# The border into the attention mixer: two chunks on the raw residual, the RMS root in the heads' norms

## Chip, cores and metric

One core of a Trainium2 chip runs the whole program in one launch. The metric is the device time of that core in microseconds; a comparison goes by the median of several runs.

## The reference, cut to what matters

Two blocks run one after the other on a residual x of 512 tokens by 1024 features. The first block ends with a post-norm (a LayerNorm), and the second begins with an RMS norm in front of its attention mixer:

```python
def _layer_norm(x, gain, bias):
    mu = jnp.mean(xf, -1, keepdims=True)
    var = jnp.mean(jnp.square(xf - mu), -1, keepdims=True)
    return (xf - mu) * lax.rsqrt(var + LN_EPS) * gain + bias
...
x = _post_norm(x, y, g3, FFN_RES, ln_gain[l, 2], ln_bias[l, 2])   # l = 1: end of the first block
...
def rmsnorm(x, g):
    return xf * lax.rsqrt(jnp.mean(xf * xf, axis=-1, keepdims=True) + EPS) * g
...
h = rmsnorm(x, g_mix[0])                                          # start of the second block
qa, ka, va, qb, ckv, qi, ki, wi = _split(h @ w_in, EVEN_SPLITS)
qa = rope(rmsnorm(qa, gq_a)); ka = rope(rmsnorm(ka, gk_a))        # by heads of 64
kb, vb = jnp.split(rmsnorm(ckv, g_kv_b) @ w_kv_up_b, 2, axis=-1)
qb = rope(rmsnorm(qb, gq_b)); kb = rope(rmsnorm(kb, gk_b))
qi = rope(qi); ki = rope(rmsnorm(ki, g_kidx)); wi = wi * (IDX_HEADS ** -0.5 * IDX_DIM ** -0.5)
```

The index scores relu(qi ki) weighted by wi choose, for every token, which keys the second half of the heads sees (the k_sel highest). A positive factor common to all scores of a token doesn't alter that choice. A head's norm removes a common factor of its input, but for its eps.

## The kernel before, in words

The residual stands transposed: XR holds 8 tiles of 128 features by 512 tokens. A chunk is 256 output columns of a weight matrix (1024 KB). SyncE loads it into one of three stage buffers, ScalarE rounds it to the high part WH (`split`), VectorE forms the low part WL (`low`), and each product is three matmuls (high x high, high x low, low x high; `mul3`) of 128 rows by 512 columns, for eight steps of k. The input of the projections is kept as a high and a low part too: HH and HL, or for the hidden layer AH and AL.

A planner (class Plan, from line 80 on) writes one list of steps; every engine then runs its own part of each step in the order of that list. `feat` and `mm2` emit a chunk's matmuls, and after every few of them `tick` (L613) lets each active generator add its next step, so that attention units, rotations and top-k rounds are spread between matmuls. `until` (L626) ticks without adding matmuls of weights until a condition holds. Temporary buffers, PSUM banks and small buffers are rings; a buffer taken again carries the event that must be over first.

Five borders of the first block use `late` (L325). While the last down projection writes the residual, `raw` (xg) scales each tile by gain times modulation into AH[1] and AL[1]. Two chunks then multiply this unnormalised residual, with a column sum of the stage's weights against two coefficient columns (`weight_sums`, L1449) after each step of k. Between these matmuls run the mean (`ln_mean`), its subtraction and the squares (`ln_sub`), the variance (`ln_var`), the root by three Newton steps (`ln_root`, twelve short VectorE instructions in `rsqrt`, L2036) and its spread over a bank (`ln_spread`). `ln_h` scales the residual and makes HH and HL, and `late_copy`, `uv_out` and `late` correct the two chunks' outputs by mean and root. `scaled` later brings XR to its final value, one tile per tick (`ln_x`).

The border into the attention mixer has no such overlap. `last_norm` (L453) computes mean, subtraction, squares, variance, root and the final residual with a second set of squares (steps ln_a and ln_last; `keep` puts nine matmuls without use into TensorE's waits). `rms_norm` (L491) then makes the mixer's root (rms_a) and h (rms_b). After it `even_mixer` (L857) projects the chunk w_kiwi (128 columns of ki twice, 4 of wi), then w_in_e 7 (qi). The squares of ki are summed (e_stat) and group(0), the norm and rotation of ki, is started behind the first half of qi: a root (g_rs), its transposes (g_turn), the scaling (g_scale) and the rotation (e_rope). `until` waits for ki; then index() (scores and top-k) and the projections of qa, ka, va follow.

## Time and profile before

| | us |
|---|---|
| median of 3 runs | 3678.25 (3675.61 to 3683.49) |
| the profiled execution | 3687.77 |
| its span, first to last instruction | 3686.4 |
| mean granted clock of TensorE | 0.974 |
| busy in the span: PE, PEld, DVE, ACT, POOL | 3572.3, 2904.3, 1882.5, 1219.3, 492.4 |

In the profile PE is TensorE's matmuls, PEld its weight loads (beside the matmuls), DVE is VectorE, ACT ScalarE, POOL GpSimd. A granted clock of 1.00 is 2.4 GHz and of 0.50 is 1.2 GHz. The end of a matmul is modelled, so the start-to-start distance of neighbours tells more than their duration.

### The profile page before, as it was taken

What the parts mean: (1) busy time and instruction counts of PE and PEld (TensorE: products, weight loads), DVE (VectorE), ACT (ScalarE), POOL (GpSimd) and SP (SyncE); (2) the same over time, 40 slices, a digit from 0 to 9 for tenths busy, and PEclk for the clock granted to TensorE, in tenths of its full rate; (3) what the DMA queues carried; (4) which work ended last, traced back from release to release, by engine and by line L of the source; (5) the groups of instructions that cost most, each with busy time, mean ns of one, the idle gap of its engine ahead of it and who ended that gap; (6) DMA issues with size and microseconds to landing.
All of it is one profiled execution on the core that took longest, in us unless ns stands there. A gap on an engine that the chain in (4) does not pass through costs nothing.

```text
span 3686.4 us, 41474 instructions
## 1 busy us (share of the span) xinstructions
PE 3572.3 (97%) x16954; PEld 2904.3 (79%) x16954; DVE 1882.5 (51%) x3255; ACT 1219.3 (33%) x1638; POOL 492.4 (13%) x432
## 2 busy tenths in 40 slices
PE   8999989999999999999999998987999999999999
PEld 7888866787888888867788886755888888888887
DVE  4545743664456454644653335686553434664333
ACT  2222461351224222552342223234442223343221
POOL 1010220110002000221110011100211111201111
PEclk9999999899999999999999998987999999999999
DMA  6444222133442444211132221100312222222221
GB/s 251 160 160 154 98 72 89 46 114 125 160 149 98 154 160 140 101 69 69 46 113 101 94 86 49 66 23 3 116 56 102 92 103 95 103 80 92 92 103 69
DMA packets 52608, 373.44 MB, mean 101 GB/s; under 512 B 5826, under 2 KB 5954, under 8 KB 9539
## 3 DMA queue, kind: packets, MB, share of 16 engines
q1 hardware_dynamic: 52418, 370.79, 28.0%
q8 instruction: 134, 2.20, 0.2%
q14 instruction: 56, 0.45, 0.0%
HBM read 368.67 MB, written 2.10 MB: 101 GB/s over the span
## 4 chain that ended last, share of the span: by engine, by line
PE 44%; DVE 4%; ACT 1%; issue 1%; POOL 0%; DVEq 0%; ACTq 0%; POOLq 0%
PE ps L1384 43%; PE ps L1409 0%; ACT s_tmp L1905 0%; DVE s_tmp L2346 0%; DVE s_tmp L2473 0%; DVE s_sm L2453 0%; DVE s_tmp L2336 0%; DVE s_sm L2344 0%; DVE s_bm L2455 0%; DVE s_tmp L2490 0%; DVE s_sm L2324 0%; DVE s_hl L2058 0%; ACT s_wh L1743 0%; DVE s_xx L2346 0%; DVE s_tmp L2486 0%
## 5 line engine op out<-in xcount | busy, mean ns | idle before, releaser
L1384 PE MATMUL ps<-s_hh,s_wh 128*128 128x512 f32 (+1 forms) x2584 | 1028.1, 398 | 16.7 <-POOL s_hl L2610 9.5
L1384 PE MATMUL ps<-s_hl,s_wh 128*128 128x512 f32 (+1 forms) x2584 | 1012.7, 392 | 0.0
L1384 PE MATMUL ps<-s_hh,s_wl 128*128 128x512 f32 (+1 forms) x2584 | 1012.5, 392 | 0.0
L2065 DVE TENSOR_TENSOR s_wl<-s_stage,s_wh 128x2048 fp32r<-128x2048 f32 (+2 forms) x278 | 625.4, 2250 | 625.8 <-ACT s_wh L1743 625.6
L1743 ACT ACTIVATE s_wh<-s_stage 128x2048 fp32r<-128x2048 f32 (+1 forms) x276 | 518.9, 1880 | 622.3 <-PE ps L1384 502.0
L1384 PEld LDWEIGHTS ps<-s_hh,s_wh 128*128 128x128 f32 (+1 forms) x2584 | 488.2, 189 | 141.5 <-issue 39.6
L1384 PEld LDWEIGHTS ps<-s_hh,s_wl 128*128 128x128 f32 (+1 forms) x2584 | 487.8, 189 | 104.8 <-issue 0.2
L1384 PEld LDWEIGHTS ps<-s_hl,s_wh 128*128 128x128 f32 (+1 forms) x2584 | 488.7, 189 | 101.4 <-issue 2.2
L1384 PE MATMUL ps<-s_ah,s_wh 128*128 128x512 f32 x1376 | 547.1, 398 | 0.0
L1384 PE MATMUL ps<-s_ah,s_wl 128*128 128x512 f32 x1376 | 537.4, 391 | 0.0
L1384 PE MATMUL ps<-s_al,s_wh 128*128 128x512 f32 x1376 | 537.0, 390 | 0.0
L2659 POOL TENSOR_TENSOR s_al<-s_tmp,s_ah 128x512 fp32r<-128x512 f32 x152 | 197.6, 1301 | 1691.6 <-ACT s_ah L1743 1691.6
L1384 PEld LDWEIGHTS ps<-s_ah,s_wl 128*128 128x128 f32 x1376 | 258.9, 188 | 54.8
L1384 PEld LDWEIGHTS ps<-s_al,s_wh 128*128 128x128 f32 x1376 | 259.4, 189 | 52.2 <-issue 1.2
L1384 PEld LDWEIGHTS ps<-s_ah,s_wh 128*128 128x128 f32 x1376 | 259.4, 189 | 52.1 <-issue 1.2
L1743 ACT ACTIVATE s_ah<-s_tmp 128x512 fp32r<-128x512 f32 x152 | 96.1, 632 | 587.6 <-DVE s_tmp L2267 328.2
L2118 DVE TENSOR_TENSOR s_xr<-ps,s_xr 128x512 f32<-128x512 f32 x96 | 66.1, 689 | 196.8 <-PE ps L1384 196.7
L2116 DVE SCALAR_TENSOR_TENSOR s_xr<-ps,s_sm,s_xr 128x512 f32<-128x512 f32 x112 | 83.8, 749 | 158.0 <-PE ps L1384 157.4
L2081 DVE SCALAR_TENSOR_TENSOR s_tmp<-s_stage,s_cond,s_tmp 128x256 f32<-128x256 f32 x381 | 156.3, 478 | 0.0
L1767 ACT ACTIVATE s_tmp<-ps 128x512 f32<-128x512 f32 x82 | 48.9, 597 | 267.2 <-PE ps L1384 267.2
L2267 DVE TENSOR_TENSOR s_tmp<-s_tmp,ps 128x512 f32<-128x512 f32 x82 | 56.2, 686 | 155.5 <-PE ps L1384 155.5
L1384 PEld LDWEIGHTS ps<-s_cc,s_tmp 128*128 128x128 f32 x764 | 103.0, 208 | 20.5 <-POOL s_tmp L2650 6.7
(434 smaller groups left out, 3752.4 us busy)
## 6 DMA issues: line engine op xcount, KB each, us to landing
s_stage<-in_w_ada SPq DMA_DIRECT2D x64, 1024.0 KB, 4.8
s_stage<-in_ffn_w_gate SPq DMA_DIRECT2D x44, 1024.0 KB, 4.8
s_stage<-in_ffn_w_up SPq DMA_DIRECT2D x44, 1024.0 KB, 4.8
s_stage<-in_ffn_down SPq DMA_DIRECT2D x32, 1024.0 KB, 4.8
s_stage<-in_w_up SPq DMA_DIRECT2D x32, 1024.0 KB, 4.7
s_stage<-in_down_m SPq DMA_DIRECT2D x32, 1024.0 KB, 4.8
s_stage<-in_w_in SPq DMA_DIRECT2D x24, 1024.0 KB, 4.8
s_stage<-in_ffn_down SPq DMA_DIRECT2D x16, 768.0 KB, 4.3
```

What stands on the lines that cost most here:

```text
L1384: return pe.matmul(out, lhs, rhs, start=start, stop=stop, skip_group_check=True)
L1743: return act.activation(out, src, ACT.Copy)
L1767: act.activation(m.tmp(q), m.bank(b), ACT.Silu).then_inc(*e.up("act_ffn", "act", pid))
L2065: ins = dve.tensor_tensor(m.WL[:, ws, a:z], m.STAGE[:, j % NS, a:z], m.WH[:, ws, a:z].bitcast(F32), ALU.subtract)
L2081: ins = dve.scalar_tensor_tensor(dst, w[:, k, :], cond, dst, ALU.mult, ALU.add)
L2116: ins = dve.scalar_tensor_tensor(x, m.bank(b), m.small(gate[0])[:, n:n + 1], x, ALU.mult, ALU.add)
L2118: ins = dve.tensor_tensor(x, m.bank(b), x, ALU.add)
L2267: dve.tensor_tensor(m.tmp(q), m.tmp(q), m.bank(b), ALU.mult).then_inc(*e.up("dve_ffn", "glu", pid))
L2659: pool.tensor_tensor(m.AL[a][:, k, :], m.tmp(q), m.AH[a][:, k, :].bitcast(F32), ALU.subtract).then_inc(*e.up("pool_a", "a.lo", av, k))
```

## The change

- At the border into the attention mixer `last_norm` and `rms_norm` are replaced: the last down projection prepares the raw residual with gain times g_mix (`ln_coef2`), and `late` does the two chunks w_kiwi (128 and 4 rows, `wide`) and w_in_e 7 on it.
- `late` is given `xq`: after each half of `ln_h`, ScalarE squares the final residual (scale and bias in the instruction) and GpSimd sums the squares (`ln_xq`).
- The mixer's h is only LayerNorm output times g_mix. The RMS root of a token isn't multiplied in. For the heads' norms it goes into their eps: mean of squares plus eps becomes eps of the head times (mean square of x plus eps) (`e_root`, small buffer ew, first four columns). For va it is a scale of the copies (`e_tcopy`, one copy per token tile, two in place of one). For the indexer it is left out, being a common factor.
- ki, wi and qi come out of `e_late`; ki's group waits for ew. The tiles of the mixer change their place in memory, as AH[1] and AL[1] now hold the raw residual while ki, qi and wi are written.

```diff
     def late(self, norm, names, wide=(P, P), xq=False):
...
-        qs = self.to_h()
-        self.add("ln_h", sid, rs, s, self.hfree, self.hv, qs, 0, 4)
-        finish(0, mean, rs)
+        self.add("ln_h", sid, rs, s, self.hfree, self.hv, self.to_h(0, 4), 0, 4)
+        sq = self.squared(sid, s, 0, None) if xq else None
+        finish(one, 0, mean, rs)
         part(1, *two, 4, 8)
-        self.add("ln_h", sid, rs, s, self.hfree, self.hv, qs, 4, NT)
+        self.add("ln_h", sid, rs, s, self.hfree, self.hv, self.to_h(4, NT), 4, NT)
+        sq = self.squared(sid, s, 4, sq[:1]) if xq else None
         self.release(two[0], ("proj", two[1] + 1))
         low = self.ahead()
         copies(two, 1)
...
+    def squared(self, sid, s, n0, acc):
+        qs = [self.tmp.take() for _ in range(1 if not acc else 0)]
+        acc = acc or qs
+        for n in range(n0 + len(qs), n0 + 4):
+            q = self.tmp.take()
+            qs.append(q)
+            self.tmp.free(q, ("ln.xf", sid, n))
+        self.add("ln_xq", sid, s, n0, qs, acc[0])
+        return acc
...
-    def even_mixer(self):
+    def even_mixer(self, norm):
...
+        def root(sq):
+            rid, y, b = self.new(), self.yr.take(), self.held.take()
+            yield
+            self.add("rms_a", rid, sq, b, y)
+            for q, _ in sq:
+                self.tmp.free(q, ("rms.st", rid))
+            self.add("e_root", rid, b, y, ew)
+            self.held.free(b, ("ew",))
+            self.yr.free(y, ("ew",))
+            done["ew"] = True
...
+        self.pipeline()
+        one, two, free, sq = self.late(norm, (("w_kiwi", 0), ("w_in_e", 7)), (P, 4), True)
+        hv, ew = self.hv, self.small.take()
...
         self.add("e_begin")
-        ch = self.take("w_kiwi", 0)
-        b, pid = self.feat(ch, 8, 132, 0, "h", hv)
...
+        for (key, t), (q, pid, su, col) in zip((("ki", 0), ("wi", 0), ("qi", 0), ("qi", 1)), one + two):
+            wi = self.tmp.take() if key == "wi" else None
+            self.add("e_late", key, t, pid, q, su, col, wi)
+            self.tmp.free(q, ("wi.c",) if key == "wi" else ("e.p", key, t))
+            if key == "ki":
+                q = self.tmp.take()
+                self.add("e_sq", key, t, None, q)
+                pend.append((q, key, t, 0))
+            elif key == "wi":
...
+        flush()
+        self.active.append(root(sq))
+        self.bg.append(lambda: "ew" in done)
+        self.bg.append(group(0, 2, [("ki", 0)]))
         self.until(lambda: ("ki", 0) in done)
...
-        total = self.last_norm(1, 2, norm)
         assert not self.fill
         self.pipeline()
...
-                self.rms_norm("g_mix", l, total)
-                self.even_mixer()
+                self.even_mixer(norm)
...
+    def ln_xq(sid, s, n0, qs, acc):
+        AG, AB = m.small(s)[:, 16:24], m.small(s)[:, 24:32]
+        for n in range(n0, n0 + 4):
+            e.wait_ge(("ln.sc", sid, n), qs[n - n0].after)
+            act.activation(m.tmp(qs[n - n0]), m.XR[:, n, :], ACT.Square, bias=AB[:, n:n + 1], scale=AG[:, n:n + 1]).then_inc(
+                *e.up("act_sq", "ln.xq", sid, n))
...
+    def e_tcopy(c, i, pid, b, ew):
+        e.wait_ge(("proj", pid), ("ew",))
+        for a in range(2):
+            ins = act.activation(m.t["va"][:, i + a, 256 * c:256 * c + 256], m.bank(b)[:, 256 * a:256 * a + 256], ACT.Copy,
+                                 scale=m.small(ew)[:, 4 + i + a:5 + i + a])
+        ins.then_inc(*e.up("act_evict", "va", c, i))
...
+    def e_root(rid, b, y, ew):
+        e.wait_ge(ew.after)
+        dve.tensor_scalar(m.small(ew)[:, 0:4], m.bank(b)[:, 0:4], 1e-6, 1e-12, ALU.mult, ALU.add).then_inc(
+            *e.up("dve_e", "ew.a"))
+        e.wait_ge(("rs", rid))
+        dve.tensor_copy(m.small(ew)[:, 4:8], m.y(y)[:, 0:4]).then_inc(*e.up("dve_e", "ew"))
+        e.wait_ge(("ew",))
...
+    def g_rs(gid, n, y, ready, ew):
+        own = 8 if gid == 2 else n
+        v, (src, w) = m.NV[:, 0:4 * n].rearrange("p (a n) -> p a n", a=4), spans((0, own), m.small(ew)[:, 0:4])
+        e.wait_ge(ready, last_rs[0])
+        ins = dve.tensor_tensor(v[:, :, 0:own], src, w, ALU.add)
+        if own < n:
+            ins.then_inc(*e.up("dve_rs", "rs.own", gid))
+            ins = dve.tensor_scalar(v[:, :, own:n], m.t["st"][:, :, own:n], 1e-6, None, ALU.add)
+        ins.then_inc(*e.up("dve_rs", "rs.v", "g%d" % gid))
+        newton("g%d" % gid, 4 * n, y)
...
+    def ln_xq(sid, s, n0, qs, acc):
+        for n in range(max(n0, 1), n0 + 4):
+            e.wait_ge(("ln.xq", sid, n), ("ln.xf", sid, n - 1) if n > 1 else ("ln.xq", sid, 0))
+            pool.tensor_tensor(m.tmp(acc), m.tmp(acc), m.tmp(qs[n - n0]), ALU.add).then_inc(*e.up("pool_sum", "ln.xf", sid, n))
```

## Rows read from the trace of the kernel before

**Rows 1.** The page's part 1, busy time, share of the span and instructions of each engine.

```profile
PE 3572.3 (97%) x16954; PEld 2904.3 (79%) x16954; DVE 1882.5 (51%) x3255; ACT 1219.3 (33%) x1638; POOL 492.4 (13%) x432
```

**Rows 2.** Windows: length, busy us of PE, PEld, DVE, ACT, POOL, clock, DMA share, GB/s.

```profile
2203.05:2237.12 34.07, 21.82 (x97) 18.05 (x96) 22.89 (x52) 18.21 (x27) 6.45 (x6) 0.64 0.08 31
2237.12:2267.40 30.28, 28.66 (x116) 19.65 (x117) 11.87 (x26) 10.26 (x13) 5.01 (x4) 0.89 0.10 35
1502.45:1535.17 32.72, 32.72 (x188) 28.17 (x186) 27.06 (x47) 16.51 (x21) 7.68 (x6) 1.00 0.10 34
```

**Rows 3.** Timeline of PE, border: start us, duration us, instruction, [idle before <-releaser].

```profile
2203.04 1.02 PE L1384 MATMUL ps<-s_tmp,s_cc 128*128 128x512 f32 x2
2225.02 5.28 PE L1384 MATMUL ps<-s_cc,s_tmp 128*128 128x1 f32 x24 [6.42 <-POOL s_tmp L2650]
2237.12 0.77 PE L1384 MATMUL ps<-s_hh,s_wh 128*128 128x512 f32 x1 [2.32 <-DVE s_hl L2058]
2243.37 0.39 PE L1384 MATMUL ps<-s_hh,s_wh 128*128 128x512 f32 x1
```

**Rows 4.** Timeline of PE around the first projection of qa.

```profile
2263.25 0.60 PE L1635 MATMUL ps<-s_cc,s_ny 128*2 128x128 f32 x4
2264.62 1.12 PE L1384 MATMUL ps<-s_rt,s_c 2*128 2x512 f32 x2 [0.77 <-DVE s_rt L2414]
2266.58 1.81 PE L1384 MATMUL ps<-s_ki,s_cc 128*128 128x512 f32 x2 [0.84 <-DVE s_ki L2424]
2267.40 1.42 PE L1384 MATMUL ps<-s_hh,s_wh 128*128 128x512 f32 x1
2268.61 0.63 PE L1384 MATMUL ps<-s_hl,s_wh 128*128 128x512 f32 x1
2270.32 0.40 PE L1384 MATMUL ps<-s_hh,s_wl 128*128 128x512 f32 x1
```

**Rows 5.** Timeline of PE at the border at 1502 us.

```profile
1502.45 0.39 PE L1384 MATMUL ps<-s_ah,s_wh 128*128 128x512 f32 x1
1503.59 0.39 PE L1384 MATMUL ps<-s_ah,s_wl 128*128 128x512 f32 x1
1535.17 0.37 PE L1384 MATMUL ps<-s_wh,s_hh 128*128 128x256 f32 x1
1539.82 0.58 PE L1384 MATMUL ps<-s_wh,s_hh 128*128 128x256 f32 x1 [1.18 <-POOL s_hl L2610]
```

**Rows 6.** Timeline of DVE behind the chunks of that border.

```profile
1540.25 2.29 DVE L2065 TENSOR_TENSOR s_wl<-s_stage,s_wh 128x2048 fp32r<-128x2048 f32 x1 [2.15 <-ACT s_wh L1743]
1545.23 0.88 DVE L2262 TENSOR_SCALAR s_sq<-s_tmp,s_sm 128x512 f32<-128x512 f32 x2
1546.03 0.88 DVE L2262 TENSOR_SCALAR s_sk<-s_tmp,s_sm 128x512 f32<-128x512 f32 x2
```

**Rows 7.** ACT and POOL there by timeline, L1811 by line (min/median/max ns).

```profile
1538.26 1.89 ACT L1743 ACTIVATE s_wh<-s_stage 128x2048 fp32r<-128x2048 f32 x1
...
1538.49 1.27 POOL L2610 TENSOR_TENSOR s_hl<-s_tmp,s_hh 128x512 fp32r<-128x512 f32 x1 [1.08 <-ACT s_hh L1815]
...
L1811 ACT ACTIVATE s_tmp<-s_xr,s_sm x40: 800/814/819, 433.8 to 1865.6; 128x512 f32<-128x512 f32 x40
```

**Rows 8.** By line: GpSimd's sums of squares, ns min/median/max.

```profile
L2640 POOL TENSOR_TENSOR s_tmp<-s_tmp x15: 1282/1290/1302, 417.7 to 1840.1; 128x512 f32<-128x512 f32 x15
```

**Rows 9.** Timeline of DVE: first and last of the 12 steps of a root.

```profile
2230.34 0.16 DVE L2040 TENSOR_SCALAR s_nv<-ps 128x4 f32<-128x4 f32 x1 [4.22 <-PE ps L1384]
2232.51 0.16 DVE L2053 SCALAR_TENSOR_TENSOR s_ny<-s_nu,s_ny 128x4 f32<-128x4 f32 x1
```

**Rows 10.** Timelines of PE and DVE: wi's transposes and their copy.

```profile
2257.34 0.41 PE L1649 MATMUL ps<-s_cc,s_tmp 4*128 4x4 f32 x4
...
2257.79 0.17 DVE L2435 COPY s_wi<-ps 128x16 f32<-128x16 f32 x1 [0.17 <-PE ps L1649]
```

**Rows 11.** Windows: the sum over 2410 to 2570 us.

```profile
sum 160.00, PE 130.42 PEld 81.58 DVE 123.66 ACT 70.53 POOL 15.67; mean PE 32.61 PEld 20.40 DVE 30.91 ACT 17.63 POOL 3.92
```

More of the change, by code:

```diff
@@ L391, in late @@
         copies(two, 1)
-        self.add("uv_out", sid, two[0], 1, uv, su)
         if low:
             self.add("low", *low)
-        finish(1, mean, rs)
+        finish(two, 1, mean, rs)
         self.held.free(uv, ("uv.out", sid, 1))
@@ L525, in ffn @@
                 if first and norm:
-                    one, two, afree[1] = self.late(norm, ((names["gate"], idx), (names["up"], idx)))
+                    one, two, afree[1], _ = self.late(norm, ((names["gate"], idx), (names["up"], idx)))
                     for (q, pid, su, col), (r, pid2, *_) in zip(one, two):
@@ L577, in ffn @@
                 if gi == len(groups) - 1 and mean and not after and not raw:
-                    self.total(mean, *total, done[:-2] if c < 3 else done)
+                    self.total(*total, done[:-2] if c < 3 else done)
                     done = done[-2:] if c < 3 else []
@@ L604, in project_out @@
             if not after and not raw:
-                self.total(mean, *total, done if last else done[:-2])
+                self.total(*total, done if last else done[:-2])
             done = done[-2:]
@@ L759, in dil_units @@
                         yield self.attend("dil", l, 2 * pr + c, i, (i + 1) * P, cell, i == 3 and c == 1)
-        one, two, free = self.late(norm, (("w_in", l * 12 + 9), ("w_in", l * 12 + 10)))
+        one, two, free, _ = self.late(norm, (("w_in", l * 12 + 9), ("w_in", l * 12 + 10)))
         for key, tiles in (("sq", one), ("sk", two)):
@@ L1400, in spread @@
         return ins
-    def keep(b, n):
-        for _ in range(n):
-            mul(b[:, 0:256], m.ident, m.CC[:, 0:256])
     def turn(b, src, n):
```

318 lines of the change are left out of this document (109 added, 209 removed).

## Prediction

> **What bounds the kernel now.** I read the page first: TensorE is busy for 97% of the span and nothing else is above 79% [rows 1]. So only places where TensorE waits, does extra work or runs at its lower clock can move the time, and the change touches one of them, the border from the last feed-forward block to the attention mixer. The table by windows comes next. From the last down projection (2203.05) to the mixer's first projection (2237.12) lie 34.07 us, in which TensorE counts as busy for 21.82 at a granted clock of 0.64; to the first projection of qa (2267.40) it is another 30.28 [rows 2]. The timeline of TensorE says what is in the first stretch: statistics, waits such as the 6.42 us for GpSimd's sum, and no projection [rows 3]. Together that is 64.36 us from 2203.04 to 2267.40, of which the projections of ki, wi and qi need only 96 matmuls at 0.228 = 21.9 (five spacings from 1502.45 to 1503.59 [rows 5]). The border loses about 42 us.
>
> The same trace holds five borders of the other kind, where two chunks multiply the unnormalised residual while the norm is computed. The fourth, at 1502 us, has the same sizes as the new one: 512 columns, eight steps of k, a first and a second chunk with column sums. From its first matmul at 1502.45 to its last column sum TensorE is never idle: 32.72 us, busy 32.72, clock 1.00 [rows 2, 5]. What follows there, a value projection, begins at once at 1535.17. These rows are the yardstick.
>
> **Part by part.** Time is counted from the last down projection, before at 2203.04, in the yardstick at 1502.45.
>
> (a) The whole of last_norm and rms_norm goes, with its nine filler matmuls (keep), and the chunk of ki and wi and the chunk of qi are done as late chunks. The four-row half of the first costs what 128 rows cost, in both kernels, since 512 columns stream through. Cost: 32.72 [rows 2, 5]. The border's upkeep inside it (column sums, mean, variance, spread) is the 10.8 above 21.9. The extra work of the down projection (the scaled residual on ScalarE and VectorE) hid under the yardstick's matmuls, and does so here.
>
> (b) Behind the chunks everything hangs on one chain. even_mixer calls until(ki done) before it emits qa's projection, and until only ticks: it adds no matmul of weights. Before, group 0 (norm and rotation of ki) was started while qi was still multiplying; now ki's group waits for a root of the sum of squares, and that for the late norm. So TensorE has nothing to hide this chain with, and each link counts.
>
> - ScalarE: its split of the next weights started at 1538.26, right after the last copies of the norm [rows 7]. Four squares with scale and bias now stand ahead of it, about 0.81 each like L1811 [rows 7]. Their fourth reuses a buffer that GpSimd frees with its first sum; that sum follows the low part at 1538.49 (1.27) and takes 1.29 [rows 7, 8], so it ends at 1541.1 and the square at about 1541.8. Shift: 3.5.
> - VectorE's low part stood at 1540.25, which becomes 1543.8; from it to the end of the late corrections are 4.98 (1540.25 to 1545.23) [rows 6]. End: 1548.8, or 46.3 on the count.
> - e_late for ki and wi, like L2262: 0.40 each (1545.23 to 1546.03 for two) [rows 6], 47.1; the four small transposes of wi, 0.41 before [rows 10] and taken as 0.6 at half clock, 47.7.
> - TensorE in its order: the sums of ki's square and of the new total, eight small matmuls each. At half clock 24 such took 5.28 [rows 3], so 16 take 3.5: 51.2. The two e_late of qi and the copies (0.17 each [rows 10]) are under it.
> - VectorE: the root of the mixer's norm, 2230.34 to 2232.67, 2.33 [rows 9]; e_root, two small ones at the 0.2 of these rows, 0.4; g_rs, another 2.4. End: 56.4.
> - From g_turn to the first matmul of qa lie 4.15 (2263.25 to 2267.40) [rows 4]; 0.3 more, as the transposes start at half clock: 60.9.
>
> Before it is 64.36. Saved: 3.5.
>
> (c) The clock. Granted clock 0.50 is 1.2 GHz of 2.4. Before, qa began after some 4 us of sparse work and had five matmuls at about 0.43 (2268.61 to 2270.32 [rows 4]); loss 1.0. Behind the emptier stretch of 34 us, fifteen spacings took 6.25 (2237.12 to 2243.37 [rows 3]) instead of 3.4; loss 2.85. After the change the sparse stretch ahead of qa is 28 us, so I take the latter: 1.9 given back.
>
> (d) Small ones. g_rs of group 2 has one VectorE instruction more, 0.2, taken as exposed. e_tcopy becomes two ScalarE copies of half the width and the eight ln_x of 0.8 move under qa; ScalarE is busy a third of the span [rows 1], so nothing. DMAs: the same chunks in the same order; each stage buffer is held until its column sums are done, as in the yardstick, and no wait on a load shows there. The wait on ew in e_tcopy is long met.
>
> Sum: -3.5 + 1.9 + 0.2 = -1.4. The profiled execution took 3687.77 (span 3686.4); by it 3686.4. The median of the runs shown lies 9.5 lower, so 3678.25 - 1.4 = **3676.9**.
>
> Two prices are not in the trace and have bounds. The squares: nothing if GpSimd and ScalarE overlap them, -3.5; 6.5 if all eight are serial, +3.0. The sums on TensorE: hidden under the late corrections down to 0, but then the e_late order still holds it, so -1.8; the other way the mixer's root could wait for GpSimd's last sum, which ends three sums after 1541.1, at 1545.0, and isn't near. The clock: between 1.0 and as much again as 2.85, -1.9 to +2.9. I keep the middle values because each comes from the same operation one border earlier.
>
> A rule to weigh. The trace shows the clock falling while TensorE waited for single copies of VectorE: 0.43 per matmul at 2268.61 after waits of 0.77 and 0.84 [rows 4]. The Trainium skill ("TensorE: Matmul & The Clock Gate", section "Loop structure matters more than you think") says that a copy out of PSUM by VectorE between groups of matmuls doesn't cost the array its warmth. By it (c) would be 0 and the sum -3.3; the rows decide against it, as here several copies stand in a chain with nothing between.
>
> **Rivals.** *Faster: the tail is covered.* If qa's projection could start behind the chunks, only waits as in the yardstick are left (1.18 the longest [rows 5], 1.4 taken) and the border falls by 64.36 - 32.72 - 1.4 = 30: 3648. Against it is until; for it only the yardstick, whose follower had no such chain. 0.04. Half-way: the squares and sums overlap and the clock is kept, -1.4 - 3.5 - 1.8 - 1.9 = -8.6: 3669.7. 0.18 together with what lies beyond.
>
> *Slower: the shifted schedule lands badly in the mixer's own thin stretch.* Units are handed out one per tick. The generator of the residual's scaling (eight ticks) now holds an active place and ScalarE at the start of the mixer, and the ring positions of all buffers change. Between 2410 and 2570 TensorE is busy for 130.42 of 160 [rows 11], waiting in turns on VectorE. It decides where units come a tick apart from the instruction that feeds them: a quarter more of these 29.6 us of idling is 7.4, with half-clock matmuls after it about 10, so 3678.25 - 1.4 + 10 = 3687. For it: that stretch waits already. Against it: all of it follows qa in tick order, and the chain through until leaves the ticks of index and groups as they were. 0.14.
>
> *The change moves the work and not the time.* The 34 us wait at 2203 becomes a 28 us wait at 2236 and the 10.8 of upkeep: that is my forecast itself.
>
> **How the numbers follow.** About 0.2% (7.4 us) can be told from no change here. Forecast with its neighbours inside 3671 to 3686: 0.62. Faster by more: 0.04 + 0.18 = 0.22. Slower by more: 0.14, and 0.02 for a longer chain than its bounds: 0.16. The range takes the low bound -8.6 and the runs' own scatter of 2.6 below, and reaches to the slower rival above: 3667 to 3687.
>
> **What would show it.** In the new trace, projections should follow the last down projection without a gap; the late part should take 32 to 33 us at clock 1.00; then TensorE should be nearly empty for 26 to 30 us, with two runs of Newton steps on VectorE and the rotation of ki last; qa should start 60 to 62 us after the last down projection, with some 14 matmuls at 0.43. The prediction is wrong if qa's matmuls stand ahead of ki's rotation, if a wait shows between the chunks, or if the idle time from 2410 to 2570 changes by over 3 us.

## The result, and the profile after

The kernel after took 3687.15 us, the median of 11 runs (3682.06 to 3692.57), against 3678.01 for the kernel before beside it (11 runs, 3674.55 to 3689.3). The ratio is 1.0021, 95% interval 1.0011 to 1.0031: slower by 0.2% in this comparison, where 3676.9 was forecast, and just outside the range of 3667 to 3687. A second comparison (r_after, below) gave 1.0005 (0.9997 to 1.0014), so that the whole times don't settle whether the change costs anything; the traces do, for one stretch. The profiled execution of after took 3683.89 (span 3682.6), which is less than the 3687.77 of the profiled execution of before, so the whole spans of the two traces don't show the loss. It has to be read stretch by stretch.

The page says that TensorE is as full as it was [rows 1]:

```profile
PE 3560.4 (97%) x16956; PEld 2893.2 (79%) x16956; DVE 1896.2 (51%) x3303; ACT 1231.1 (33%) x1654; POOL 503.9 (14%) x439
```

The windows of after, with the columns of [rows 2]: the late chunks, then from their end to the first projection of qa.

```profile
2195.64:2228.36 32.72, 32.72 (x187) 25.20 (x185) 26.41 (x45) 18.43 (x24) 10.33 (x9) 1.00 0.09 33
2228.36:2260.67 32.31, 8.42 (x31) 5.47 (x30) 17.89 (x50) 14.51 (x19) 10.74 (x7) 0.58 0.27 98
```

The timeline of TensorE in after, over the second of them. It answers to [rows 3, 4].

```profile
2228.01 0.50 PE L1374 MATMUL ps<-s_sm,s_stage 128*128 128x2 f32 x4
2245.75 0.59 PE L1614 MATMUL ps<-s_cc,s_xe 4*128 4x4 f32 x4 [17.24 <-DVE s_xe L2359]
2246.27 3.57 PE L1374 MATMUL ps<-s_cc,s_tmp 128*128 128x2 f32 x16
2254.89 1.01 PE L1600 MATMUL ps<-s_cc,s_ny 128*2 128x128 f32 x4 [5.05 <-DVE s_ny L2014]
2256.67 2.07 PE L1374 MATMUL ps<-s_rt,s_c 2*128 2x512 f32 x2 [0.77 <-DVE s_rt L2380]
2259.58 2.08 PE L1374 MATMUL ps<-s_ki,s_cc 128*128 128x512 f32 x2 [0.84 <-DVE s_ki L2390]
2260.67 1.42 PE L1374 MATMUL ps<-s_hh,s_wh 128*128 128x512 f32 x1
2261.88 0.63 PE L1374 MATMUL ps<-s_hl,s_wh 128*128 128x512 f32 x1
```

The late chunks follow the last down projection without a gap, 32.72 us at clock 1.00, to the hundredth what the yardstick said. Then comes the nearly empty stretch. From the last down projection to qa it is 2260.67 - 2195.64 = 65.03 us, where it was 64.36 before and 60.9 was forecast.

What filled the gap of 17.24 us is on the other engines. VectorE in after, the two scales in the second half of ln_h, the low part of the next weights, and the first of the two e_late:

```profile
2226.96 1.52 DVE L2157 TENSOR_SCALAR s_hh<-s_xr,s_sm 128x512 fp32r<-128x512 f32 x1
...
2230.78 1.53 DVE L2157 TENSOR_SCALAR s_hh<-s_xr,s_sm 128x512 fp32r<-128x512 f32 x1
...
2239.85 2.29 DVE L2026 TENSOR_TENSOR s_wl<-s_stage,s_wh 128x2048 fp32r<-128x2048 f32 x1 [6.07 <-ACT s_wh L1708]
...
2244.83 0.48 DVE L2361 TENSOR_SCALAR s_ki<-s_tmp,s_sm 128x512 f32<-128x512 f32 x1
```

GpSimd and ScalarE there, by their timelines: three sums of squares and the next low part of h, then the last square of the second half and the copy that makes the high part of the weights.

```profile
2225.47 4.13 POOL L2610 TENSOR_TENSOR s_tmp<-s_tmp 128x512 f32<-128x512 f32 x3
2230.77 1.27 POOL L2576 TENSOR_TENSOR s_hl<-s_tmp,s_hh 128x512 fp32r<-128x512 f32 x1 [1.17 <-ACT s_hh L1775]
```

```profile
2237.14 0.81 ACT L1782 ACTIVATE s_tmp<-s_xr,s_sm 128x512 f32<-128x512 f32 x1 [0.41 <-POOL s_tmp L2610]
2237.86 1.89 ACT L1708 ACTIVATE s_wh<-s_stage 128x2048 fp32r<-128x2048 f32 x1
```

VectorE's part of the split (`low`) starts at 2239.85, which is 44.2 on the count from the last down projection; the forecast had 41.3, and the yardstick without squares 37.8 [rows 6]. Every later link carries that lateness on.

Three marks measure the kernels below, each read from a timeline: T0 (the end of the last down projection, 2.8 us ahead of the first subtraction of the norm in kernels with the border of before and 4.7 in those with the new one), the rotation of ki on TensorE (the row `s_ki,s_cc`), and the first matmul on s_mh, with which the mixer's attention is done. "Clock lost" is length times (1 - granted clock), summed over 36 equal windows between rotation and s_mh; part of it falls on idle time and costs nothing.

| us | T0 to rotation | rotation to s_mh | clock lost in it | T0 to s_mh |
|---|---|---|---|---|
| before | 63.5 | 355.4 | 32.3 | 419.0 |
| before, second profile (r_before) | 62.6 | 355.0 | 32.1 | 417.6 |
| after | 63.9 | 357.2 | 36.3 | 421.2 |
| after, second profile (r_after) | 63.9 | 357.3 | 36.3 | 421.2 |

So the change costs 0.4 to 1.3 us in the border and about 2.0 in the mixer behind it, 2.2 to 3.6 us together. Ahead of T0 nothing moved that can be put down to it: from the first subtraction of the border before it to T0 both second profiles took 368.8 us, after too, and before 367.6. Behind s_mh, to the end of the span, it is 1064.4 and 1062.9 us in the two profiles of before, and 1065.8 and 1065.7 in those of after. That would be 1.3 to 2.9 us more, but the kernels below lie anywhere from 1062.6 (aw_f1) to 1068.1 (e_cover, x_mix) there, whatever their border, so it isn't counted as the change's. With it the traces would give 3.6 to 6.5 us from T0 to the end.

### The profile page after: what moved, and what is told of

It is laid out like the page before. It is cut to its first block and busy times, and to the rows that moved or that the text cites. A ratio compares the mean times of both kernels' runs of the same rounds, so it can differ in the third digit from the quotient of the medians.

```text
span 3682.6 us, 41575 instructions
## 1 busy us (share of the span) xinstructions
PE 3560.4 (97%) x16956; PEld 2893.2 (79%) x16956; DVE 1896.2 (51%) x3303; ACT 1231.1 (33%) x1654; POOL 503.9 (14%) x439
## 5 line engine op out<-in xcount | busy, mean ns | idle before, releaser
L1374 PE MATMUL ps<-s_hh,s_wh 128*128 128x512 f32 x2552 | 1013.7, 397 | 14.3 <-POOL s_hl L2576 9.3
L1374 PE MATMUL ps<-s_hl,s_wh 128*128 128x512 f32 x2552 | 998.9, 391 | 0.0
L1374 PE MATMUL ps<-s_hh,s_wl 128*128 128x512 f32 x2552 | 998.6, 391 | 0.0
L2026 DVE TENSOR_TENSOR s_wl<-s_stage,s_wh 128x2048 fp32r<-128x2048 f32 (+1 forms) x276 | 623.2, 2258 | 618.5 <-ACT s_wh L1708 618.3
L1374 PEld LDWEIGHTS ps<-s_hh,s_wh 128*128 128x128 f32 x2552 | 482.5, 189 | 136.3 <-issue 37.0
L1374 PEld LDWEIGHTS ps<-s_hh,s_wl 128*128 128x128 f32 x2552 | 482.2, 189 | 103.1
L1374 PE MATMUL ps<-s_ah,s_wh 128*128 128x512 f32 x1408 | 561.5, 399 | 0.0
L1374 PEld LDWEIGHTS ps<-s_hl,s_wh 128*128 128x128 f32 x2552 | 482.7, 189 | 99.3 <-issue 2.2
L1374 PE MATMUL ps<-s_ah,s_wl 128*128 128x512 f32 x1408 | 549.9, 391 | 0.0
L2186 DVE TENSOR_TENSOR s_tmp<-ps,s_c 128x512 f32<-128x512 f32 x64 | 44.1, 689 | 119.0 <-PE ps L1374 105.4
```

The lines of the kernel that those rows point to most:

```text
L1374: return pe.matmul(out, lhs, rhs, start=start, stop=stop, skip_group_check=True)
L2026: ins = dve.tensor_tensor(m.WL[:, ws, a:z], m.STAGE[:, j % NS, a:z], m.WH[:, ws, a:z].bitcast(F32), ALU.subtract)
L2186: dve.tensor_tensor(x, m.bank(b), m.RB, ALU.mult).then_inc(*e.up("dve_act", "act", pid))
```

## The experiments

**Both kernels once more.** The text of r_before and of r_after is that of the kernels before and after, unchanged.

> The kernel before, once more, as a second trace and as the measure of its own scatter. Every theory expects a ratio of 1.000 (interval within 0.2%). In its trace the border from the last down projection to qa's first projection should again take 64.4 us, as it is a chain of waits; the stretches between the five late borders, which moved by -3 and -6 us between the two traces at hand with no change of code, should move again if that is the granted clock's phase.

> The changed kernel once more. Theory A (the border explains it): the border again takes 65.0 us against 64.4, the rest is scatter, and the ratio comes down to 1.000 to 1.001. Theory B (the mixer behind the border became slower): the border takes 65.0, the stretch from qa's first projection to the end is 3 us or more above that of the kernel before again (it was 1421.9 against 1419.0), and the ratio stays at 1.002. Theory C (the code ahead of the border, down projections with the scaled residual): the stretch from the mixer's late border at 1830 us to the last down projection is longer by 1 us again (368.7 against 367.6).

Measured: r_before 3681.9 us, ratio to before 1.0007 (0.9996 to 1.0018); r_after 3682.66, ratio 1.0005 (0.9997 to 1.0014). A program compared with itself came out at 1.0007, and the change that had stood at 1.0021 at 1.0005. In this second comparison the two kernels can't be told apart. The table above has their traces: the border and the mixer repeat to 0.1 us in after, and the down projections ahead of the border are the same in both kernels, so theory C falls. The border of before didn't repeat: to qa's first matmul it is 63.1 us in r_before, where 64.4 was expected, since fewer of its matmuls ran at half clock. What else differs between profiles of one program lies in the blocks ahead: the stretch between the norms at 416 and 743 us took 327.7 us in the profile of before and 324.5 in r_before. The loss that the traces can place, 2.2 to 3.6 us or 0.06 to 0.10%, is less than the first comparison's 0.2%; what makes up the rest isn't shown, and part of it can be the scatter of one comparison to the next (0.07% for the program against itself).

**Without the mixer's root (x_noroot).** Its sums on TensorE and its Newton steps go; eps and va's scale come from a constant, so the output isn't computed.

```diff
-            self.add("rms_a", rid, sq, b, y)
-            self.add("e_root", rid, b, y, ew)
+            self.add("e_root", ew)
```

> The changed kernel with the mixer's root left out: no sum of the squares over features on TensorE, no Newton steps, the eps and the scale of va come from a constant vector (that part of the result is not computed). Squares and their sums stay. My theory (every link of the tail is exposed in full): the border becomes shorter by the sum's eight matmuls at half clock (1.8) and twelve Newton steps (2.4), 4 to 4.5 in all, to 60.5, and the whole by as much. Rival (the clock decides: a border shorter by some us leaves the same half-clock stretches elsewhere): the border shrinks, the whole does not.

Measured: 3681.0 us, ratio 0.9998 (0.999 to 1.0007). T0 to rotation 61.1, 2.8 less than in after, where I had put 4 to 4.5. The timeline of TensorE in x_noroot has eight small matmuls instead of sixteen and a gap of 2.83 instead of 5.05; from wi's turn to the rotation it is 9.9 us instead of 13.8, so the root costs 3.9.

```profile
2244.52 0.58 PE L1610 MATMUL ps<-s_cc,s_xe 4*128 4x4 f32 x4 [16.72 <-DVE s_xe L2354]
2245.03 1.87 PE L1370 MATMUL ps<-s_cc,s_tmp 128*128 128x2 f32 x8
2249.73 1.01 PE L1596 MATMUL ps<-s_cc,s_ny 128*2 128x128 f32 x4 [2.83 <-DVE s_ny L2010]
```

What is missing between 3.9 and 2.8 was lost ahead of the root, in the late chunks, where nothing was changed. They took 34.32 us at clock 0.95 in x_noroot (2193.32 to 2227.64), 32.72 at 1.00 in after. Behind the sixteen matmuls of the variance the next ones ran 0.43 us apart instead of 0.23:

```profile
2208.72 1.99 PE L1370 MATMUL ps<-s_cc,s_tmp 128*128 128x1 f32 x16
2210.56 0.78 PE L1370 MATMUL ps<-s_ah,s_wh 128*128 128x512 f32 x1
2211.14 0.63 PE L1370 MATMUL ps<-s_al,s_wh 128*128 128x512 f32 x1
```

And the mixer took 359.0 us in place of 357.2, although the order of ticks is that of after. Of the 3.9 only 1.1 arrived at s_mh (420.1).

**One square and no sums (x_onesq).** ScalarE does one square instead of eight, GpSimd none of the seven sums.

```diff
-        for n in range(n0, n0 + 4):            # ln_xq on ScalarE
+        for n in range(n0, n0 + 1):
-        for n in range(max(n0, 1), n0 + 4):    # ln_xq on GpSimd
-            pool.tensor_tensor(m.tmp(acc), ..., ALU.add)
+        pass
```

> The changed kernel with one square on ScalarE instead of eight and none of GpSimd's seven sums; the mixer's root is taken from that one square, so the output is not the reference's. Theory A (the squares and sums slow the second half of ln_h and push VectorE's split and the late corrections by 5 to 6 us together against the yardstick): the split of the next weights starts 38 to 40 us after the last down projection instead of 44.2, and from there to the ki rotation it is 58 to 60 us instead of 64.0. Theory B (the squares are hidden, the delay is that of the ring or of the bank): the split within 1 us of 44.2 and the rotation within 1 of 64.0.

Measured: T0 at 2200.1. VectorE in x_onesq, the two scales that took 1.52 and 1.53 in after, and the low part of the weights:

```profile
2231.40 0.55 DVE L2154 TENSOR_SCALAR s_hh<-s_xr,s_sm 128x512 fp32r<-128x512 f32 x1
...
2233.78 0.55 DVE L2154 TENSOR_SCALAR s_hh<-s_xr,s_sm 128x512 fp32r<-128x512 f32 x1
...
2238.38 2.29 DVE L2023 TENSOR_TENSOR s_wl<-s_stage,s_wh 128x2048 fp32r<-128x2048 f32 x1 [2.06 <-ACT s_wh L1705]
```

The low part stands at 38.3 on the count instead of 44.2, and the rotation at 58.1 instead of 63.9. Theory A holds with its numbers: squares and sums together cost the border 5.9 us. And yet the program took 3691.14 us in its one run, since the mixer behind took 367.8 us, 10.6 more.

**Eight squares and no sums (x_nosum).** Only GpSimd's seven additions go.

```diff
-            pool.tensor_tensor(m.tmp(acc), ..., ALU.add)    # ln_xq on GpSimd
-            self.tmp.free(q, ("ln.xf", sid, n))
+            self.tmp.free(q, ("ln.xq", sid, n))
```

> The changed kernel with all eight squares on ScalarE but without GpSimd's seven sums; the mixer's root is taken from the first square alone, so the output is not the reference's. With one square and no sums the split of the next weights started 38.3 us after the last down projection, with all of them 44.2. Theory A (GpSimd's sums are the larger part: while one of them runs, VectorE's scale into s_hh takes 1.5 us instead of 0.55, twice, and ScalarE's fourth square waits for one): the two scales are back at 0.55, the split comes at 41 to 42, and the ki rotation at 61 to 62 instead of 64.0. Theory B (the squares on ScalarE are all of it): split at 44, rotation at 63.5 to 64.

Measured: one run, 3689.67 us; T0 at 2201.4. The timelines of VectorE, ScalarE and GpSimd in x_nosum:

```profile
2232.71 0.55 DVE L2157 TENSOR_SCALAR s_hh<-s_xr,s_sm 128x512 fp32r<-128x512 f32 x1
...
2235.09 0.55 DVE L2157 TENSOR_SCALAR s_hh<-s_xr,s_sm 128x512 fp32r<-128x512 f32 x1
...
2242.64 2.29 DVE L2026 TENSOR_TENSOR s_wl<-s_stage,s_wh 128x2048 fp32r<-128x2048 f32 x1 [5.01 <-ACT s_wh L1708]
```

```profile
2237.69 3.06 ACT L1782 ACTIVATE s_tmp<-s_xr,s_sm 128x512 f32<-128x512 f32 x4
```

```profile
2235.54 1.27 POOL L2576 TENSOR_TENSOR s_hl<-s_tmp,s_hh 128x512 fp32r<-128x512 f32 x1 [4.39 <-ACT s_hh L1775]
```

The low part stands at 41.2, the rotation at 61.0: theory A, inside its numbers. So the 5.9 us are 2.9 of ScalarE's squares (3.06 for four, on the path) and 3.0 of GpSimd's sums. Most of the sums' harm is done without anybody waiting for their result: with them VectorE's two scales into s_hh take 1.52 and 1.53 us, without them 0.55 each, which is 1.9 of the 3.0 by itself. Only the first of them runs beside a sum (2226.96, in the three sums from 2225.47 to 2229.60). The second runs beside GpSimd's low part of h, which both kernels have: in after the two start together (2230.78 and 2230.77), in x_nosum VectorE starts 0.45 ahead (2235.09 and 2235.54) and isn't held up. Of the rest, 0.41 is ScalarE's last square waiting for a sum. The mixer behind took 360.2 us in x_nosum, 3.0 more than in after. The Trainium skill (SBUF — State Buffer, section "SBUF: two separate sides") says that VectorE and GpSimd share a pair of ports under an exclusive lock, and that a VectorE operation in a two-port mode is blocked for as long as GpSimd's instruction holds it; the 1.52 and 1.53 against 0.55 of this case agree.

**The gaps filled with matmuls (x_warm).** 86 matmuls whose sums nobody reads, in a free bank, 68 ahead of the turn of wi and 18 behind the root's sums.

```diff
+        self.add("warm", warm, 1, 68, hv)      # behind the late chunks
+            self.add("warm", warm, 2, 18, hv)  # in root, behind rms_a
+    def warm(b, k, n, hv):
+        for _ in range(n):
+            ins = mul(m.bank(b), m.HH[:, 0, 0:P], m.HH[:, 0, :])
```

> The changed kernel with 86 matmuls more whose sums nobody reads (128x512, into a bank that is free there): 68 between the last late chunk and the turn of wi, 18 behind the root's sums. They fill the gaps of 17.2 and 5.0 us at 0.227 us each and change no other step. Theory A (the clock that falls to half in the gap is what the border lost against the forecast): granted clock 1.00 up to qa, the root's sums 1.8 instead of 3.6 us, the turn and the rotation 4.4 instead of 5.8, nothing of the 2.2 us lost in the first 5 us behind the rotation; 64.0 becomes 60.5 to 61.5 from the last down projection to the ki rotation, 357.2 becomes 355 behind it, together 4.5 to 5.5 us: 0.9985 of the changed kernel. Theory B (the steps wait for VectorE and ScalarE, not for TensorE's clock): less than 1.5 us together.

Measured: 3682.35 us, ratio 1.0009 (0.9994 to 1.0023); T0 to rotation 63.1, rotation to s_mh 358.1, together 421.2 as in after. The timeline of TensorE in x_warm:

```profile
2248.94 0.41 PE L1624 MATMUL ps<-s_cc,s_xe 4*128 4x4 f32 x4 [1.81 <-DVE s_xe L2369]
2249.31 2.94 PE L1378 MATMUL ps<-s_cc,s_tmp 128*128 128x2 f32 x16
2252.11 6.54 PE L1378 MATMUL ps<-s_hh 128*128 128x512 f32 x18
2258.49 0.60 PE L1610 MATMUL ps<-s_cc,s_ny 128*2 128x128 f32 x4
2259.86 1.12 PE L1378 MATMUL ps<-s_rt,s_c 2*128 2x512 f32 x2 [0.77 <-DVE s_rt L2390]
```

The turn is back at 0.60 and 1.12 us, and in the first 5 us behind the rotation the clock is 1.00 (0.56 in after). But the clock fell in the root's small sums all the same (0.98 in the window 2249.00 to 2250.00, 0.50 from there to 2256.00), so the second batch took 6.54 us where its gap has 5.05, and the transposes waited for it. Theory B by its number, less than 1.5 us together, though not by its reason: the border gained 0.8, the mixer took back 0.9. Its clock losses, 35.7 us, are near those of after (36.3), although it began at full clock. So the mixer's 2 us don't go away with a warm start, as I had thought they would.

**The filling with the index let out faster (aw_f1, af2).** Both let out the sixteen top-k rounds of tile 1 two to a tick; af2 has 76 and 10 filling matmuls instead of 68 and 18.

```diff
                 for r in range(16):
                     self.add("ix_top", i, r, s)
-                    yield
+                    if r % 2 or i != 1:
+                        yield
```

> The changed kernel with the 86 filling matmuls and with the index let out two top-k rounds to a tick for tile 1. If the clock's gain in the border (about 5 us) and the pace's gain in the mixer (4.3 us from the ki rotation to s_mh when the kernel before had it alone) are independent, the stretch from the last down projection to s_mh falls from 421.2 to 411 to 413 us and the whole is 0.997 to 0.998 of the kernel before, better than either kernel. Rival: the mixer's thin stretch takes one of them back (its clock falls to 0.7 there in any case): 415 to 418, 0.999.

> As the kernel with 86 filling matmuls and the doubled rounds of tile 1, but with 76 matmuls in the first gap, up to the turn of wi, and 10 in the second. There TensorE sat idle for 1.8 us before the turn of wi, its clock fell to half about 1 us after, in the root's small sums, and the second batch took 5.97 instead of 4.1 us at that clock and overran its gap. Theory A (that 1.8 us hole lets the clock fall): granted clock 1.00 to qa, 60 to 61 us from the last down projection to the ki rotation instead of 61.5, and 410.2 becomes 409 to s_mh. Theory B (the small sums of 2 columns are as good as a hole for the clock, however the gap ahead of them is filled): the clock still falls within 5 us of the turn of wi, but the shorter second batch no longer overruns; 61 to 61.5.

Measured: aw_f1 3674.35 us, ratio 0.9992 (0.998 to 1.0004), T0 to s_mh 410.2 (61.5 and 348.7); af2 3679.7, ratio 0.9995 (0.9983 to 1.0006), T0 to s_mh 413.5 (61.8 and 351.7). The stretch of aw_f1 came out even below the 411 to 413 expected for independent gains. But it isn't the sum of the gains as they were measured singly: x_warm alone gained nothing to s_mh, and the faster index alone 4.3 to 5.7 (b_f1, below), against 11.0 here. The whole shows less than the 0.997 to 0.998 expected (with 15 us between its lowest and highest run, that stays open). The border's steps are those of x_warm, the 1.81 us hole ahead of wi's turn included, and yet it is 1.6 us shorter; TensorE in aw_f1:

```profile
2248.25 1.92 PE L1379 MATMUL ps<-s_cc,s_tmp 128*128 128x2 f32 x16
2250.03 5.97 PE L1379 MATMUL ps<-s_hh 128*128 128x512 f32 x18
```

Here the small sums ran at full clock (1.92 us, 2.94 in x_warm), and the clock fell in the second batch only, 3.4 us behind the start of wi's turn and not 1.0 (0.66 in the window 2251.00 to 2252.00). The timeline of TensorE in af2:

```profile
2251.76 0.41 PE L1625 MATMUL ps<-s_cc,s_xe 4*128 4x4 f32 x4
2252.14 1.92 PE L1379 MATMUL ps<-s_cc,s_tmp 128*128 128x2 f32 x16
2253.91 2.52 PE L1379 MATMUL ps<-s_hh 128*128 128x512 f32 x10
2259.11 0.60 PE L1611 MATMUL ps<-s_cc,s_ny 128*2 128x128 f32 x4 [2.67 <-DVE s_ny L2025]
2260.48 2.07 PE L1379 MATMUL ps<-s_rt,s_c 2*128 2x512 f32 x2 [0.77 <-DVE s_rt L2391]
```

With no hole ahead of the turn of wi, the sums and the second batch (0.25 a matmul) ran at full clock, as the second batch did in neither of the other two. That speaks for the hole of 1.8 us, but on one profile, and the small sums are no witness, being as fast in aw_f1 with the hole. Behind the next hole, 2.67 us after the shorter batch, the clock fell to half. So it is neither theory, and at 61.8 the border was no shorter than in aw_f1: the chain runs through VectorE, and the slower turn and rotation took back what the batch had given.

**The chain covered by qa (e_cover).** until(ki done) goes; the turn of wi, ki's statistics, the root and ki's group run as a unit of their own, six ticks late, beside the projections of qa and ka, and qa's first chunk takes its two tiles in turn.

```diff
-        self.active.append(root(sq))
-        self.bg.append(group(0, 2, [("ki", 0)]))
-        self.until(lambda: ("ki", 0) in done)
+        self.active.append(tail(sq, wi, kq))
+        self.bg.append(lambda: ("ki", 0) in done)
```

> The changed kernel, but without the wait for ki ahead of the projections: qa's first chunk starts right behind qi's, with its two tiles in turn, and wi's transposes, ki's statistics, the mixer's root, ki's norm and its rotation are handed out by ticks under the chunks of qa (the first after six ticks); ki's statistics have columns of their own. The index starts some 11 ticks later. My theory (the tail behind the late chunks is what ate the gain): the 32.3 us between the last late matmul and qa's first fall to under 3, and the time falls by 20 to 30 us against the kernel before, unless the later index gives some of it back in the stretch before the second half of the heads; then 8 to 20. Rival (the tail is not what costs: the down projections, the squares, or the later stages do): the time stays above that of the kernel before.

Measured: 3679.15 us, ratio 0.9994 (0.9985 to 1.0003). qa's projections begin where the late chunks end, and the only wait there is one of 5.64 us, so the border's tail of 32 us is gone, and T0 to s_mh still is 415.3, only 5.9 less than in after. Two things lie between. The tail was never 32 us of waiting: TensorE had 8.4 us of work in it, 23.9 were idle. And TensorE waited elsewhere instead: from T0 to s_mh it is idle for 56.6 us in after and for 48.2 in e_cover, as much as in the kernel before (48.4). The longest group of TensorE's waits in e_cover from 2190 to 2640 (total, times, longest), and the window with VectorE at its fullest (35.99 of 40):

```profile
PE ps L1403 <- DVE s_tmp L2290: 19.6, 18, 8.3
```

```profile
2470.00:2510.00 40.00, 23.21 (x106) 18.89 (x104) 35.99 (x101) 11.46 (x29) 5.12 (x4) 0.62 0.00 0
```

The index starts when ki is rotated. Its 48 top-k rounds on VectorE now start late and end at 2502, and the second half of the heads waits for their mask, 8.25 us at 2503.68. The expectation had allowed for a later index, but with a gain of 8 to 20 us over the kernel before left; the stretch has 2.3 to 3.7.

**The index's pace (e_fast, e_f4, b_f1).** The cover with two rounds to a tick for tiles 1 and 2 (e_fast); with four for tile 1 and two for tile 2 (e_f4); and the kernel before with two for tile 1 and nothing else changed (b_f1).

```diff
-                    yield
+                    if r % 2 or i == 3:                               # e_fast
+                    if r % 4 == 3 or i > 1 and r % 2 or i == 3:       # e_f4
+                    if r % 2 or i != 1:                               # b_f1
+                        yield
```

> The cover again (the root and its group in a tail that runs beside qa, ka), with the index now let out two top-k rounds to a tick for its tiles 1 and 2 (16 ticks fewer). Theory A (what was gained by the cover was given back because the index started about 11 ticks later and its 48 rounds on VectorE end late: 8.3 us of TensorE's wait on L2290, and a thin stretch of 23.2 busy us in 40): the index ends at least 15 us earlier than the 2501.8 of the cover alone, the wait on its mask goes, and from the last down projection to the first s_mh it takes 10 to 20 us less than the 415.3 of the cover alone; whole 0.994 to 0.997 of the kernel before. Theory B (VectorE is full there with splits and rounds, the order of its rounds is no matter): that stretch within 3 us of 415.3, the waits of TensorE move to the splits of weights; whole 0.998 to 1.000.

> The cover with a still quicker index: four top-k rounds to a tick for tile 1, two for tile 2, one for tile 3 (4 ticks fewer than the cover with two for both). If VectorE still has room there, the stretch from the last down projection to s_mh falls from 408.9 to 405 to 408, whole 0.9975 of the kernel before. If VectorE is full (46.2 of 50 us busy in its fullest stretch), 409 to 412: the rounds then hold back the splits of the weights, and TensorE waits for those.

> The kernel before, untouched at the border, with the index let out two top-k rounds to a tick for tile 1 alone (8 ticks fewer): the control for the pace of the index. If the late index is a matter of the cover only, this one takes from the last down projection to the first s_mh the 417.6 to 419.0 us of the kernel before, within 2, and the whole is 0.999 to 1.001. If the pace of the index was already the bound in the kernel before, that stretch is 4 to 8 us shorter (0.998). If doubled rounds crowd out the weight splits on VectorE, it is 3 or more longer.

Measured: e_fast 3674.48 us, ratio 0.9984 (0.9975 to 0.9993), T0 to s_mh 408.9; e_f4 3674.88, 0.998 (0.997 to 0.9991), 410.1; b_f1 3675.45, 0.9986 (0.9977 to 0.9995), 413.3. By the instructions on s_bm the last MAX8 of the index starts at 2500.2 in e_cover, 2474.6 in e_fast and 2454.7 in e_f4. The same window in e_fast:

```profile
2470.00:2510.00 40.00, 31.68 (x154) 23.39 (x152) 22.55 (x86) 15.20 (x40) 4.50 (x4) 0.66 0.00 1
```

TensorE is busy for 31.68 instead of 23.21 and the long wait is gone (1.8 us is the longest left of its group), by theory A; but it gave 6.4 us, less than the 10 to 20 expected, the whole stayed above the 0.994 to 0.997 expected, and still quicker rounds gave none. b_f1 shows that the pace was already worth 4.3 to 5.7 us in the kernel before. By the stretch to s_mh that is about half of what e_fast gained on the kernel before (8.7 to 10.1), by the ratios most of it (0.14 of 0.16%), so the cover's own share stays open. All three are faster than the kernel before beside them, and not told apart from one another; none was measured in one comparison with the kernel after.

**The change's edits inside the mixer (x_mix).** The border of before; va in two scaled copies, eps from a buffer (here of constants), group 2's sum in two steps.

```diff
-            self.add("g_rs", gid, n, y, list(st["ev"]))
+            self.add("g_rs", gid, n, y, list(st["ev"]), ew)
-                self.add("e_tcopy", c, i, pid, b)
+                self.add("e_tcopy", c, i, pid, b, ew)
```

> The border of the kernel before, with the edits that the change makes inside the mixer alone: va copied by ScalarE in two scaled copies instead of one, the eps of the heads' norms read from a small buffer (here filled with the constants 1e-6 and 1.0, so no mixer's root is needed), group 2's sum in two operations, that buffer held until they are done. Theory A (those edits cause the mixer's 2 us): from the ki rotation to the first s_mh 357, as in the changed kernel (357.2, 357.3), against 355.4 and 355.0 before. Theory B (what starts under qa does: the residual's scaling ln_x, the ring's position and the schedule shifted by the border): 355 to 355.6.

Measured in its one run: rotation to s_mh 354.5 us, clock lost 32.4: theory B. The edits inside the mixer cost nothing in that stretch. The run as a whole took 3688.79 us, with 1068.1 behind s_mh, as long there as the longest of all kernels (e_cover); one run can't say what that is.

**The index some ticks later in the kernel before (b_tick1, b_tick2, b_tick3).**

```diff
         def index():
+            for _ in range(1):      # 2, 3
+                yield
             for t in range(2):
                 rope(("qi", t), ("e.p", "qi", t))
```

> The kernel before with the index let out one tick later, nothing else. Theory A (the mixer's thin stretch answers to the order in which its units meet, by the share of it that TensorE spends at half clock): from the ki rotation to the first s_mh 355.0 to 355.4 becomes something else by 2 us or more, either way, and nearly all of the difference is time lost to the clock (32.0 us before). Theory B (only the time at which the index ends counts): 1 tick later, 0.5 to 1.5 us longer.

> The kernel before with the index let out two ticks later. Theory A: off 355 by 2 us or more, in no order with the runs of one and three ticks, with the difference in time lost to the clock. Theory B: 1 to 3 us longer, between those two.

> The kernel before with the index let out three ticks later. Theory A: off 355 by 2 us or more, in no order with the runs of one and two ticks, with the difference in time lost to the clock. Theory B: 1.5 to 4.5 us longer, the longest of the three.

One window each, over the stretch from the rotation to s_mh, with length, TensorE's busy time, granted clock, DMA share and GB/s. r_before:

```profile
2258.49:2613.50 355.01, 321.72 (x1583) 0.91 0.12 45
```

b_tick1:

```profile
2256.54:2614.00 357.46, 323.97 (x1583) 0.90 0.13 45
```

b_tick2:

```profile
2263.13:2631.10 367.97, 332.59 (x1583) 0.87 0.13 43
```

b_tick3:

```profile
2256.57:2614.20 357.63, 323.59 (x1582) 0.90 0.13 45
```

x_onesq:

```profile
2258.23:2626.00 367.77, 334.45 (x1583) 0.87 0.12 41
```

With nothing changed but a tick, the mixer takes 357.5, 368.0 and 357.6 us in place of 355, in no order, with 35.7, 47.8 and 34.0 us lost to the clock in place of 32.1, while TensorE's idle time stays at 33 to 35 us. This is theory A, on one run each (3679.18, 3696.1 and 3680.57 us, beside 3680.72 for the kernel before). It makes two open findings look alike without showing their cause: after's 357.2 with 36.3 lost is near the value of one and three ticks, and the 367.8 with 49.1 lost of x_onesq near that of two. The values are not just these two, though: x_warm has 358.1, x_noroot 359.0, x_nosum 360.2. A change ahead of the mixer can shift it by 2 to 13 us, whatever the change itself is worth. What selects the value isn't settled. It isn't the order of ticks alone, which x_noroot and x_onesq share with after; the times at which the steps meet, the ring positions and the new places of the mixer's tiles in memory were not tried by themselves. Chance from run to run it isn't either: both profiles of before agree to 0.4 us, both of after to 0.1.

## Why the prediction was wrong, by its own steps

- (a) The late chunks: right, 32.72 us for 32.72, no gap, clock 1.00.
- (b) First link, the shift by the squares, 3.5: **the step that failed.** It measured 6.4 against the yardstick (44.2 for 37.8), and by the two kernels without them 5.9: 2.9 for the squares and 3.0 for GpSimd's sums. The prediction followed ScalarE's queue and one wait for a sum at the end. It did not ask what GpSimd's three sums of the first half run beside, which is the second half of ln_h on VectorE, nor what that moves: one scale is held up by a sum, the next by a low part that it now meets. [rows 7] had shown GpSimd only with its low parts. The bound given for the squares, +3.0 over the value taken, did hold the shift, but for another reason, eight serial squares.
- The sums on TensorE at half clock: right, 3.57 for 3.5. Root, e_root and g_rs: right, from 2249.88 to 2254.84 for 5.1. The root as a whole costs 3.9 by x_noroot, from wi's turn to the rotation.
- From g_turn to qa, 4.45: mis-sized. It took 5.78 (2254.89 to 2260.67), since all of it ran at half clock and not the first transposes alone. With the 2.9 above this makes the 4.1 by which 65.0 exceeds 60.9.
- (c) The clock behind the border, +1.9: wrong in size. Full clock was back after six matmuls and not after fourteen, so against the profiled before, with its own five slow ones [rows 4], it is about 0; against r_before, which has none, 2.2, counted from the rotation. Against the profiled before, the errors of 1.3 and 1.9 partly cancel, by luck.
- (d) The edits inside the mixer: right, nothing (x_mix); the 0.2 for g_rs of group 2 wasn't seen. That ln_x under qa is free was not tried by itself. But the sum put nothing else for the mixer behind the border, and there about 2 us were lost.
- The rule of the Trainium skill that was weighed ("TensorE: Matmul & The Clock Gate", section "Loop structure matters more than you think"): with nothing but copies of VectorE between them, the groups of small matmuls ran at half clock in both profiles of after, where the clock was at half already behind the hole of 17.2 us. In the unchanged border of before it fell at 2266.9, behind the waits of 0.77 and 0.84 with no such hole ahead, and in that of r_before it held through the same waits. So these rows decide neither for the rule nor against it, and a clock term of 0, which the rule gave, is what came out against before.
- The slower rival, the shifted schedule in the mixer: it got 0.14 and is what happened, in small. By x_mix, x_warm and the runs of ticks its mechanism is the likely one, but it isn't shown for after itself. Its price of 10 is near the largest value seen (x_onesq, b_tick2), and after got 2. Its place was wrong: the idle time from 2410 to 2570 changed by 0.6 us only (131.00 busy for 130.42 [rows 11]); the loss is in the granted clock over the whole mixer.
- The faster rival, the cover: of its 30 us TensorE had been idle for 23.9, and 12.3 was the most that arrived at s_mh, with a quicker index besides (e_fast; 5.9 without). The index, which the prediction had left out, was next.

The sum that the traces support: +0.4 to +1.3 in the border and about +2.0 in the mixer, 2.2 to 3.6 us (0.06 to 0.10%) instead of -1.4. The measured 1.0021 and 1.0005 lie on both sides of it. The first link alone, put right by its 2.9, would have brought the forecast from 3676.9 to 3679.8; the 3687.15 of the first comparison is past anything that the traces account for.

## What to carry to other kernels

An operation whose result nobody waits for can still have a price: look at what is on VectorE while GpSimd's new work runs, and at what starts together with GpSimd's old work once that has shifted. Where a stretch has holes of a microsecond or more and TensorE's clock falls in them, a gain or a loss ahead of it can be smaller than the jump between its schedules; shift the kernel by a tick or two, with nothing else changed, and see how far it jumps before any gain of that size is believed. And before a chain is covered, count how much of it is really idle, and ask what its result starts: here the index, which then ended late enough for TensorE to wait for its mask.

## What the hardware showed unexpectedly

- VectorE's scale of a 128x512 tile takes 0.55 us alone (2231.40 in x_onesq, 2232.71 in x_nosum), 1.52 beside a sum on GpSimd (2226.96 in after) and 1.53 beside a low part that GpSimd started 0.01 us ahead of it (2230.78); when VectorE started 0.45 ahead of the low part it took 0.55 (2235.09 in x_nosum).
- In x_warm TensorE fell to half its clock (1.2 GHz) behind an idle 1.81 us, in the small matmuls that followed; in aw_f1, with the same steps, these ran at full clock (2.4 GHz) and it fell in the batch behind them. Without that hole both ran at full clock (af2), and it fell behind the next one, of 2.67 us. Two profiles of one program can differ too: before fell to half at ki's rotation (2266.9), r_before did not.
- The clock can fall without any wait: in x_noroot TensorE was busy for all 34.32 us of the late chunks, and behind sixteen matmuls of one column the clock was 0.50 (2211.00 to 2213.00), which made them 1.6 us longer. In after the same steps ran at 1.00 throughout.
- A mixer of some 355 us has values apart by 2.5 and 13 us under shifts of its schedule by single ticks, and the difference goes with what is lost to the lower clock: 35.7 (one tick) and 47.8 us (two) in place of 32.1.
